# A hybrid decoder trunk with expert retrieval: the making of the next step's expert indices moved from a step's second slot into its first

## What is computed

```python
x = x + W_out( sig(gA)*(A W_oA) + sig(gB)*(B W_oB) + sig(gM)*(M W_oM) )   # mixers: gated MLP, causal convolution, attention
# retrieval (_peer): 8 heads, 2 x 128 keys, 16384 experts
v1, i1 = lax.top_k(s[:, :, 0], 16);  v2, i2 = lax.top_k(s[:, :, 1], 16)
cand = v1[..., :, None] + v2[..., None, :]              # 256 sums for each token and head
cv, ci = lax.top_k(cand, 16)                            # the sixteen best sums
e1 = take_along_axis(i1, ci // 16);  e2 = take_along_axis(i2, ci % 16)
eid = e1 * 128 + e2                                     # the experts' indices
g = softmax(cv)
hid = gelu(einsum('bd,bhkd->bhk', xb, u_tab[eid]))      # a row of u for each chosen expert
y = einsum('bhk,bhkd->bd', g * hid, v_tab[eid])         # and a row of v
```

## Time and profile before

| | |
|---|---|
| median of three runs | 2299.56 us |
| the profiled execution | 2291.08 us |
| its span, first to last instruction | 2289.3 us |
| TensorE matmuls, busy | 1632.4 us (71%) |
| VectorE, busy | 1577.9 us (69%) |
| ScalarE, busy | 664.2 us (29%) |
| GpSimd, busy | 667.9 us (29%) |
| moved by DMA | 898.66 MB, mean 393 GB/s |
| of it by the gathers' queue | 604.02 MB, 63.8% of 16 engines' span |
| of it by SyncE's queue | 292.68 MB, 32.1% |

### The profile page before, as it was taken

One profiled execution on the slowest core, in us unless ns is written; L12 is line 12 of the kernel. 1 busy time (PEld: TensorE's weight loads), 2 busy tenths in 40 slices (PEclk: granted clock), 3 DMA queues, 4 the chain that ended last, 5 costly groups with the idle time before them and its releaser, 6 DMA issues.

```text
span 2289.3 us, 30931 instructions
## 1 busy us (share of the span) xinstructions
PE 1632.4 (71%) x10746; PEld 1057.0 (46%) x10746; DVE 1577.9 (69%) x4192; ACT 664.2 (29%) x1662; POOL 667.9 (29%) x594
## 2 busy tenths in 40 slices
PE   8999977669997557688779647765999854333333
PEld 8865666337885236455534414543878620000000
DVE  3545268779766666877775668966875686876774
ACT  2112134331233332423123323342123333322222
POOL 0000032222332432333223333231322354444442
PEclk9999979778998679889889757987989865555555
DMA  8687699999999999999999999999999999999996
GB/s 303 264 298 253 234 389 421 419 420 390 410 421 420 421 421 421 422 406 420 421 391 422 420 421 421 421 414 401 401 385 420 405 406 421 422 421 421 421 422 272
DMA packets 127290, 898.66 MB, mean 393 GB/s; under 512 B 16064, under 2 KB 16768, under 8 KB 18848
## 3 DMA queue, kind: packets, MB, share of 16 engines
q0 software_dynamic: 82944, 604.02, 63.8%
q1 hardware_dynamic: 44192, 292.68, 32.1%
HBM read 888.53 MB, written 8.11 MB: 392 GB/s over the span
## 4 chain that ended last, share of the span: by engine, by line
PE 35%; DMA 33%; DVE 19%; ACT 4%; issue 4%; DVEq 3%; POOL 1%; SPq 0%; another core or an unknown queue 0%; POOLq 0%; ACTq 0%
DMA uv<-uv_in,idx_u 24%; PE bank L1423 16%; DVE uv L1321 8%; DMA ring<-w_in 7%; PE bank L1920 5%; PE bank L1429 5%; PE bank L1678 5%; DVE yB L913 2%; DMA ring<-cache_in 2%; POOL uv L462 1%; DVE x L1342 1%; ACT L514 1%; ACT diag L830 1%; DVEq L908 1%; PE bank L1862 1%
## 5 line engine op out<-in xcount | busy, mean ns | idle before, releaser
L462 POOL DMA_INDIRECT uv<-uv_in,idx_u x576 | 656.5, 1140 | 1394.3 <-PE bank L1920 1095.6
L1321 DVE CUSTOM_DVE_ANT_0 uv<-uv,xrep 128x1024 f32<-128x1024 f32 x576 | 681.3, 1221 | 204.6 <-DMA uv<-uv_in,idx_u 197.5
L1920 PE MATMUL bank<-uv,diag 128*32 128x512 f32 x2304 | 426.0, 821 | 517.8 <-ACT diag L830 514.3
L1423 PEld LDWEIGHTS bank<-xnT,ring 128*128 128x128 f32 x3200 | 441.0, 203 | 80.1 <-issue 66.2
L1423 PE MATMUL bank<-xnT,ring 128*128 128x160 f32 (+1 forms) x3200 | 462.9, 306 | 6.9 <-DMA ring<-w_in 5.3
L1920 PEld LDWEIGHTS bank<-uv,diag 128*32 128x32 f32 x2304 | 53.2, 123 | 736.0 <-ACT diag L830 661.5
L514 ACT ACTIVATE pick<-pick 128x2 f32<-128x2 f32 (+1 forms) x324 | 70.0, 216 | 1051.0 <-DVE pick L1321 1048.8
L913 DVE SCALAR_TENSOR_TENSOR yB<-ext_p,small,yB 128x128 f32<-128x128 f32 x960 | 279.5, 353 | 20.4 <-issue 1.1
L514 ACT ACT_TABLE_LOAD x140 | 179.6, 1283 | 2.4
L830 ACT ACTIVATE diag<-gated_fold,pick 128x32 f32<-128x32 f32 x576 | 154.2, 315 | 9.5 <-ACT pick L514 0.2
L1678 PE MATMUL bank<-ring,xnT 128*128 128x512 f32 x192 | 88.0, 613 | 0.0
(11 more groups left out here) (205 smaller groups left out, 1700.4 us busy)
## 6 DMA issues: line engine op xcount, KB each, us to landing
ring<-w_in SPq DMA_DIRECT2D x220, 1024.0 KB
ring<-cache_in SPq DMA_DIRECT2D x32, 1024.0 KB
uv<-uv_in,idx_u POOLq DMA_INDIRECT x576
uv<-w_in SPq DMA_DIRECT2D x4, 1024.0 KB, 13.5
ext_s<-state_in SPq DMA_DIRECT2D x2, 1088.0 KB, 10.7
convs_out<-ext_s SPq DMA_DIRECT2D x2, 1088.0 KB
ext_s<-mem_in SPq DMA_DIRECT2D x2, 1024.0 KB, 18.8
memk_out<-phase SPq DMA_DIRECT2D x2, 1024.0 KB, 11.8
```

What stands on the lines that cost most here:

```text
L462: nc.gpsimd.indirect_dma_start(out=uvbuf[2 * b + i], out_offset=None, in_=uv_in, in_offset=bass.IndirectOffsetOnAxis(ap=ids[:, c:c + 1], a ...
L1321: ins = V.tensor_tensor_reduce(out=u, in0=u, in1=xrep[gg % 2][:, :], scale=1.0, scalar=0.0, op0=ALU.mult, op1=ALU.add, accum_out=hid[:, c: ...
L1423: ins = MM(out, w[:, k, P * b:P * (b + 1)], rhs(k), start=k == 0, stop=k == KB - 1)
L1920: ins = MM(vbank[gg % 2][c:c + 32, :], diag[:, t % 4, i], uvbuf[2 * b + i][:, D + 512 * n:D + 512 * (n + 1)], start=first, stop=last)
```

## The change

In VectorE's loop the call of `pick_experts` goes from the branch of slot 1 to the branch of slot 0, directly behind `pick_pairs`. Slot 1 has no branch of its own any more and falls through to `elif mix`, so that its mixers' parts come ahead of `scale_fold(s, 1)`; the later call of `mix` in that slot finds nothing left to do. No instruction is added or removed.

```diff
@@ -1382,7 +1382,6 @@
                     dots(t)
                     if k == 0 and s + 1 < NSTEP:
                         pick_pairs()
-                    elif k == 1 and s + 1 < NSTEP:
                         pick_experts(s + 1, layer(s + 1))
                     elif k == 3 and s + 1 < NSTEP:
                         gates(s + 1)
```

## The result

The changed kernel took 2299.52 us (median of 19 runs, 2296.45 to 2305.55), the kernel before 2295.88 us beside it (19 runs, 2291.34 to 2300.81): ratio 1.0016, 95% interval 1.0009 to 1.0023, or 3.6 us slower. The change costs 3 to 4 us; the forecast had 6.8.

A forecast was written before the change was run, and what follows sets the result against it. The prediction took the DMA engines as the bound, so only places where they run dry count. Its terms, 1.7 (step 0), 3.4 (step 3) and 1.7 (step 22), sum to 6.8 us over 2299.6, giving 2306.4 us; range 2296 to 2315.

The forecast's parts named there:

- Earlier indices release nothing: GpSimd's gathers: those of a running step wait for buffers freed by values matmuls, not for the indices.
- Steps 26 to 34: Steps without mixers: slot 6's gather goes out 3.4 us later, but the DMA engines are full; cost nothing.
- Step 0, 1.7: Fifth slot's gather 3.4 us later, DMA engines dry as much longer; lasting loss 0 to 3.4, half taken.
- a shrinking second place: Sign: if the second dry place of the DMA engines shrinks, the sum of step 0 is wrong.
- the ring's loads: Weight loads from 356.26, 32.85 us of waits, sharing the engines with late gathers; taken as speaking for a lasting loss.
- Step 3, 3.4: Values of slot 1 and the gather behind them 3.4 us late, nothing absorbing it; loss 3.4, bounds 0 and 3.4.
- The dry place 3.4 longer: Sign in step 3: the DMA engines stand dry 3.4 us longer.
- Step 22, +1.7: Slot 1's values 3.4 us late, TensorE's 1.72 wait absorbs part; 1.7 us lost up to the gather, bounds 0 and 3.4.
- Time lost stays lost: After each dry place the DMA engines are full up to the next, so the loss of 6.8 us is kept.
- The rival of no change: Steps 0 and 22 give their shift back; 3.4 us or less left, 2300 to 2303; chance 0.39.
- The clock's rival: Longer TensorE gaps in steps 0 and 22 halve its clock, 3.0 us more in each; 2312.4 us; chance 0.12.
- The rival of idle time filled: In five steps (6, 8, 9, 11, 13) the block fills VectorE's idle time; 8.4 us faster, 2291.2; chance 0.11 with rival four.

The follow-up runs named there:

- e1: Kernel before with the indices made in slot 0 in step 0 alone: 2299.55 us, 1.0012 of the kernel before.
- e18: Kernel before with the indices made in slot 0 in step 0 alone, run once more: 2298.20 us, 1.0011 of the kernel before.
- e2: Kernel before with the indices made in slot 0 in step 3 alone: 2298.59 us, 1.0011 of the kernel before.
- e6: Kernel before with the indices made in slot 0 in step 22 alone: 2291.47 us, 0.9994 of the kernel before.
- e17: The changed kernel once more, against the kernel before: 2298.93 us, ratio 1.0013.
- e13: The changed kernel again, against the kernel before of the same group: 2298.92 us, ratio 1.0017.
- e3: Kernel before with the indices made in slot 0 in all steps but 0 and 3: 2297.05 us, 1.0003 of the kernel before.
- e4: The kernel before itself, unchanged, for the scatter between executions: 2295.52 us, ratio 0.9996.
- e16: Kernel before with the indices made in slot 0 in step 3 alone, run again: 2297.84 us, 1.0013 of the kernel before.
- e5: Kernel before with the gather of step 0's fifth slot also waiting for the values of slot 2: 2300.46 us, 1.0030 of the kernel before.
- e12: Kernel before with best sums (slot 0) and indices (slot 1) behind the mixers' parts of their slots, all steps: 2300.34 us, 1.0038 of the kernel before.
- e14: Kernel before with eight idle copies ahead of each of two ScalarE score copies of portion 0: 2297.18 us, 1.0011 of the kernel before.

## Why the prediction was wrong

**Earlier indices release nothing: right.** 18 of the 20 waits that bore the indices' name lost it, and GpSimd waited more under the other one (+86.0 for -67.4).

**Steps 26 to 34 at nothing: right**, 401.5 to 402.0 us for 402.3 and 402.6.

**Step 0, 1.7: not refuted, and in part luck.** The shift itself came as forecast: the wait of TensorE is 5.30 for 5.4, the gather 3.5 later for 3.4. The dry place grew by 3.7; with step 0 alone the one in step 3 fell by 1.8 (e1) and by 2.0 (e18: 20 x 0.07 = 1.4 left). The net 1.7 to 1.9 is the half that the prediction took, but the half was the middle of 0 to 3.4 and not worked out; what sets it here is that the next place can give back only what is dry there. The prediction also named a shrinking second place as a sign that its sum for step 0 is wrong. It did shrink, by about the half that the prediction had already taken off, so that the sign does not tell against 1.7 but only against the full 3.4. The time can't confirm 1.7: the medians of e1 and e18 are 2.8 and 2.5 with 2 us to either side, and the distance to step 5 says 1.0 and 0.7. Whether the ring's loads have a part in it was not tested, so neither was what the prediction drew from the turns of the queues. And all of this holds with the stalls of ScalarE; without them there is no dry place in step 0.

**Step 3, 3.4: right in its mechanism, a little large.** TensorE's wait is 8.53 where 8.7 was forecast; these are the changed kernel's rows beside the earlier trace rows:

```profile
541.65 1.93 PE L1919 MATMUL bank<-uv,diag 128*32 128x512 f32 x8 [8.53 <-ACT diag L830]
...
553.86 1.06 PE L1919 MATMUL bank<-uv,diag 128*32 128x512 f32 x8
...
555.73 0.94 POOL L462 DMA_INDIRECT uv<-uv_in,idx_u  x1 [8.62 <-PE bank L1919]
```

From the values of slot 1 to those of slot 2 it is 12.21 us for 13.05 before, so that of the 3.3 more ahead of them 2.4 reach the gather, counted from the values of slot 0 (520.90 before, 527.51 here); the prediction had the full 3.4 there. Alone the step cost 2.5 and 3.0 us by the medians, and 4.0 and 3.1 in the distance from step 0 to 5 (339.0 and 338.2 for the mean of 335.1). The two places together make 5.0 there in the changed kernel; the prediction had 5.1. "The dry place 3.4 longer" was right in e2 (2.8) but only 0.8 in the changed kernel, because step 0's half was given back in the same place.

**Step 22, +1.7: this is the step that failed.** The prediction said that the dots of slot 2 stay in place, that the 1.72 us of waiting absorb half of the 3.4, and that 1.7 "is left in the chain up to the gather at 1687.74". The first two are right, and the 1.7 was still there at the values of slot 2 (1.9 in e6). What failed is the stretch from there to the gather: it was taken to run as long as before, and the clock behind the absorbed wait was put at nothing. With that wait gone the same work ran at 1.00 instead of 0.50 and took 8.0 us of work and 0.8 of waiting in place of 12.7. So the gather came 2.0 us *earlier* relative to slot 0 in e6, and 1.1 in the changed kernel (1665.08 of the values of slot 0 to 1697.78, 32.7 for 33.8; 1.9 and 2.0 in e17 and e13). The dry place fell from 4.4 to 2.3 in the changed kernel, to 2.3 in e6 and to 12 x 0.17 = 2.0 in e3. The prediction had weighed the clock as a rival and only with a plus sign. The Trainium skill (TensorE: Matmul & The Clock Gate, Part 1) has the rule that an idle array falls to half its clock; the trace agrees as to the waits of 1.72 and 3.71, with 0.50 to 0.55 behind them. What the prediction left out is the other side: without the wait of 1.72 the clock stayed full.

**"Time lost stays lost" was right only in part.** Steps 5 to 26 gave back 1.2 us on average and the last stretch 0.6, and the prediction had +1.7 and 0 there. With 5.0 - 1.2 - 0.6 = 3.2 for the 6.8 that were summed, 3.6 is the difference. The 1.7 of step 22 that did not come is about half of it; its gain of 1.1 to 2.0 up to the gather would make most of the rest, but about 1 us of that goes again in step 24, and step 3 came out smaller by 0.4 to 0.9 us (medians) than its term. That the -1.2 comes from step 22 and not from elsewhere is argued from its dry place and e6, not shown by a median: e6's interval reaches from -3.9 to +1.1.

**The number was carried onto a weak base.** The median of three runs, 2299.56, stood 3.7 above the median of 19, so that even with the right sum the forecast would have been 2303. That 2299.52 lies in the stated range of 2296 to 2315 therefore says little. Said as a difference, the forecast was 6.8 for 3.6. Two slips of the text change nothing: slice 21 of the earlier trace rows has 391 and not 390, and 15 less 6.8 is 8.2.

**The rivals.** The rival of no change came nearest, with 0 to 3.4 left for a measured 3.0 to 4.1 and part of step 0 given back in step 3. But in step 22 it counted on idle time to take up the shift, and most of what took it up was the clock. The clock's rival, 3.0 more each in steps 0 and 22, fell: in step 22 the 32 matmuls behind the lengthened wait took 5.61 in e6, where it forecast 9.3, and 6.25 before, and in step 0 the clock of the windows is 0.78 with and without the change, and the 32 matmuls behind the gap took 6.49 where they had taken 6.26. The rival of idle time filled was right in its mechanism and wrong in its gain: VectorE's wait ahead of the dots of slot 1 of step 8, 4.09 us in the earlier trace rows, is now 0.75, and those dots come as they did. No time came of it up to step 26 that could be told from the scatter, which fits the reason given against this rival, that the wait itself is for the DMA; it was not tested by itself.

```profile
814.34 1.23 DVE L1321 CUSTOM_DVE_ANT_0 uv<-uv,xrep 128x1024 f32<-128x1024 f32 x1 [0.75 <-DMA uv<-uv_in,idx_u]
```

## What to carry to other kernels

In a kernel that the DMA engines bound, only the places where they run dry can gain or lose. List them first, in every stretch; follow each shift to the next wait for something that has *not* moved. If that wait is longer than the shift, the sum ends there, as at slot 2 of step 0; if it is shorter, the rest goes on, and the work behind has to be priced anew, at the clock that it will have. Here a wait of 1.72 us that vanished gave back 4.7 us of TensorE's work, more than the 3.5 us by which the moved block had made TensorE late. And take a releaser's name in a table of waits as a question; here 67 us of waits lost the name of the indices, and GpSimd waited no less.

## What the runs showed of the hardware

- ScalarE's two stalls of 2.5 us at 288 to 294 us, with the releaser "remote", stand in ten profiles (before, after, e1 to e4, e13, e16 to e18) and in none of the eight of e5 to e12, which ran on two other chips, with the same code at the same place. Behind them the slots start about 6.6 us later after the first gather. Eight idle copies ahead of the fifth and sixth scores took their place in e14, and the time rose by only 2.5 us (0.5 to 4.4). What the stall waits for the profile doesn't say.
- Behind a wait of TensorE of 1.72 us (before, step 22) the granted clock was 0.50 and 16 matmuls took 4.45 us; without the wait (e6) it was 1.00 and they took 2.44.
- The medians of the kernel before in the five groups were 2295.8, 2292.6, 2293.0, 2294.8 and 2295.7 us, the lower two where the stalls are missing: as large a difference as the whole effect of the change, so that kernels of different groups can't be compared to better than that.
- Two executions of one kernel differ by 3.9 us from the first gather to the end (2004.6 and 2008.5 us, before and e4), nearly all of it between steps 5 and 26 (1233.7 and 1237.1 us).
